# Channel mixer of a two-layer decoder on one core: order of the first half-size products' operands, of the reloads of `a`, and of the loads of the parked `x`

## The reference, cut to what matters

```python
def finish(x, m, w_o, g_post_mix, g_pre_ffn, g_post_ffn, w_gate, w_up, w_down):
    x = x + rmsnorm(m @ w_o, g_post_mix)
    h = rmsnorm(x, g_pre_ffn)
    f = (jax.nn.silu(h @ w_gate) * (h @ w_up)) @ w_down
    return x + rmsnorm(f, g_post_ffn)
```

## Time and profile before

| | |
|---|---|
| median of three executions | 3031.42 us (3029.75 to 3041.99) |
| profiled execution, its own time | 3035.28 us |
| span from first to last instruction | 3033.5 us |
| mean granted TensorE clock | 0.988 |
| TensorE (PE) busy | 2925.0 us, 96% of the span |
| VectorE (DVE) busy | 1804.6 us, 59% |
| ScalarE (ACT) busy | 1370.4 us, 45% |
| GpSimd (POOL) busy | 1169.5 us, 39% |
| half-size products, layer 0 and layer 1 | from 821 us and from 2316 us |
| down projections, layer 0 and layer 1 | from 1243 us and from 2738 us |

### The profile page before, as it was taken

The page is one execution under the profiler, slowest core; times in us unless marked ns, Lnnn a source line. Parts: engine busy times, 40 slices in busy tenths (PEclk is TensorE's granted clock), DMA queues, the critical chain, the costliest instruction groups (busy, mean ns, idle before and its releaser), DMA issues. The chain is left out here.

```text
span 3033.5 us, 53219 instructions
## 1 busy us (share of the span) xinstructions
PE 2925.0 (96%) x20726; PEld 2548.6 (84%) x20726; DVE 1804.6 (59%) x3496; ACT 1370.4 (45%) x2616; POOL 1169.5 (39%) x864
## 2 busy tenths in 40 slices
PE   8999999999899999999999999999998999998998
PEld 6777756669799999999977777665797999998997
DVE  5579675557754555444555887654678555444552
ACT  4366625564443333444333765355654333333442
POOL 3002031315465655454700201313355656654542
PEclk9999999999999999999999999999999999999999
DMA  5120325652312222676521112356512222237653
GB/s 182 40 65 29 100 100 185 232 193 60 101 57 85 85 84 73 194 215 196 150 79 46 50 34 94 142 182 232 180 60 76 77 79 82 64 115 239 186 169 103
DMA packets 391922, 357.57 MB, mean 118 GB/s; under 512 B 33281, under 2 KB 353690, under 8 KB 391674
## 3 DMA queue, kind: packets, MB, share of 16 engines
q1 hardware_dynamic: 371194, 282.86, 30.5%
q0 software_dynamic: 20480, 71.32, 6.8%
HBM read 299.66 MB, written 54.44 MB: 117 GB/s over the span
## 5 line engine op out<-in xcount | busy, mean ns | idle before, releaser
L750 PE MATMUL ps<-w_in_slots,hT 128*128 128x256 f32 (+1 forms) x2048 | 447.0, 374 | 4.9 <-PEq L214 3.2
L750 PEld LDWEIGHTS ps<-w_in_slots,hT 128*128 128x128 f32 x2048 | 373.1, 192 | 60.1 <-issue 10.2
L2901 POOL TENSOR_TENSOR t_lo<-t_raw,t_hi 128x512 fp32r<-128x512 f32 x200 | 272.6, 1365 | 259.7 <-ACT t_hi L2715 259.7
L2414 PE MATMUL ps<-a_lo,wd_hi 128*128 128x352 f32 x1056 | 348.6, 330 | 16.2 <-DVE a_lo L3057 11.7
L2414 PE MATMUL ps<-a_hi,wd_hi 128*128 128x352 f32 x1056 | 342.4, 324 | 0.0
L2414 PE MATMUL ps<-a_hi,wd_lo 128*128 128x352 f32 x1056 | 342.1, 324 | 0.0
L2929 POOL TENSOR_TENSOR wd_lo<-wd_raw,wd_hi 128x1024 fp32r<-128x1024 f32 x96 | 212.6, 2222 | 232.3 <-ACT wd_hi L2756 232.2
L3023 DVE TENSOR_TENSOR t_raw<-w_pair,w_pair 128x512 f32<-128x512 f32 x120 | 134.0, 1117 | 270.1 <-PE ps L2520 270.1
L2520 PE MATMUL ps<-s_lo,t_hi 128*128 128x264 f32 x960 | 274.9, 286 | 3.7 <-issue 3.7
L2520 PE MATMUL ps<-s_hi,t_lo 128*128 128x264 f32 x960 | 274.6, 286 | 0.0
L2520 PE MATMUL ps<-s_hi,t_hi 128*128 128x264 f32 x960 | 274.2, 286 | 0.0
(11 more groups left out here) (408 smaller groups left out, 7116.0 us busy)
## 6 DMA issues: line engine op xcount, KB each, us to landing
wd_raw<-in_w_down SPq DMA_DIRECT2D x192, 192.0 KB, 3.1
wd_raw<-in_w_down SPq DMA_DIRECT2D x96, 256.0 KB, 3.3
a_in<-apark SPq DMA_DIRECT2D x132, 176.0 KB, 3.9
w_pair<-in_w_gate SPq DMA_DIRECT2D x40, 512.0 KB, 5.1
w_pair<-in_w_up SPq DMA_DIRECT2D x40, 512.0 KB, 4.9
w_in_slots<-in_w_in SPq DMA_DIRECT2D x18, 1024.0 KB, 5.4
apark<-a SPq DMA_DIRECT2D x40, 264.0 KB, 2.1
apark<-t_up SPq DMA_DIRECT2D x40, 264.0 KB, 4.2
```

Source lines behind the costliest of these rows:

```text
L750: ins = pe.matmul(ps[:m, bank[i], 0:w], hT[:, k, cols(n)], W[:, g % 2, k, 0:w], start=(k == 0), stop=(k == KC - 1))
L2414: ins = pe.matmul(bank(b), w, x, start=first and i == 0, stop=end and i == 2)
L2901: pool.tensor_tensor(t_lo[e][:, :, :], t_raw[e][:, :, :] if len(src) > 1 else src[0], t_hi[e][:, :, :].bitcast(F32), ALU.subtract).then_in ...
```

## The change

It touches four places of `channel`. The matmuls and their order stay as they are.

1. `s5` becomes the first combination. Its sum is made by VectorE ahead of the sixth `invert` of the norm part, its rounding stands first in ScalarE's list, and its rest moves from GpSimd to VectorE. `multiply_up(2)` and `(3)` move behind the first weight sums, `multiply_up(4)` and `(5)` ahead of the rest of `s1`.
2. On ScalarE the copies of the first three products and the rounding of weight 4 move ahead of the rounding of `s7` and `s6`. On VectorE the weight sums 5, 6 and 7 are put between the last rests.
3. On SP the reloads of `a` numbers 12 to 19 move ahead of the second and third parking of the last pair and ahead of the weights of turn 1; ScalarE rounds group 0 of turn 1 after all 22 blocks of `a`.
4. The parked x comes back in 12 pieces of 128 x 2 x 352 elements, one at the end of each of the turns 3 to 6, 9 to 12 and 17 to 20, instead of three thirds in turn 2.

```diff
-    combs = {"s1": (A11, A22, ALU.add), "s5": (A11, A12, ALU.add), "s2": (A21, A22, ALU.add), "s7": (A12, A22, ALU.subtract),
+    combs = {"s5": (A11, A12, ALU.add), "s1": (A11, A22, ALU.add), "s2": (A21, A22, ALU.add), "s7": (A12, A22, ALU.subtract),
...
@@ sync
             park_pair(PAIRS - 1, 0)
+            for x in range(NX, NX + 4):
+                load_a(x)
+            park_pair(PAIRS - 1, 1)
+            for x in range(NX + 4, FC - 2):
+                load_a(x)
             sp.wait_ge(p_mm, NP - 2)
             load_down(1, 0)
-            park_pair(PAIRS - 1, 1)
-            for x in range(NX, NX + 3):
-                load_a(x)
-            load_down(1, 1)
-            load_down(1, 2)
             park_pair(PAIRS - 1, 2)
-            for x in range(NX + 3, FC - 2):
-                load_a(x)
             park_pair(PAIRS - 1, 3)
             load_a(FC - 2)
             load_a(FC - 1)
+            load_down(1, 1)
+            load_down(1, 2)
...
+            x1_at = (3, 9, 17)
...
-                if u == 2:
+                if u == x1_at[0]:
                     sp.wait_ge(p_mm, NP)
                     for n in range(3):
-                        for m in range(3):
-                            sp.wait_ge(parked[m], 32 if m == 2 else 16)
-                        sp.dma_start(third(hT, n), third(xpark, n)).then_inc(x1_in[n], 16)
+                        sp.wait_ge(parked[n], 32 if n == 2 else 16)
+                for n in range(3):
+                    if x1_at[n] <= u < x1_at[n] + 4:
+                        k = slice(2 * (u - x1_at[n]), 2 * (u - x1_at[n]) + 2)
+                        sp.dma_start(hT[:, k, of(n)], xpark[:, k, of(n)]).then_inc(x1_in[n], 16)
@@ tensor, product
-                if q == 0 and pos == 3:
-                    pe.wait_ge(s5_lo_done, 1)
-                elif q == 0 and pos >= 2:
-                    pe.wait_ge(comb_lo_done, max(1, pos - 2))
+                if q == 0 and pos >= 2:
+                    pe.wait_ge(comb_lo_done, max(2, pos - 1))
@@ scalar
+            round_comb("s5")
             silu(4)
             silu(5)
             round_comb("s1")
             for m in range(3):
                 round_weight(m)
-            round_comb("s5")
             silu(8)
             act.wait_ge(mm, 9)
             round_weight(3)
             silu(10)
-            for n in ("s2", "s7", "s6"):
+            round_comb("s2")
+            keep_product(0, 0)
+            round_weight(4)
+            keep_product(0, 1)
+            keep_product(0, 2)
+            for n in ("s7", "s6"):
                 round_comb(n)
-            for done in range(1, NP + 1):
+            for m in (5, 6):
+                round_weight(m)
+            for done in range(4, NP + 1):
...
-            round_a(0, *range(12, 15))
+            round_a(0, *range(12, FC))
             round_down(1, 0)
-            round_a(0, *range(15, FC))
@@ gpsimd
-            for m in range(3):
+            for m in range(4):
                 rest_of_weight(m)
-            pool.wait_ge(comb_hi_done, comb_nth["s5"])
-            pool.tensor_tensor(comb_lo["s5"][:, :, :], comb_raw["s5"][:, :, :], comb_hi["s5"][:, :, :].bitcast(F32), ALU.subtract).then_inc(s5_lo_done, 1)
-            rest_of_weight(3)
@@ vector
+                if th == 2:
+                    dve.wait_ge(x_add, 3 * (KC - 1))
+                    sum_comb("s5")
                 invert(2 * th + 2)
...
-            for u in range(4):
-                multiply_up(u)
+            multiply_up(0)
+            multiply_up(1)
             sum_comb("s1")
             sum_weight(0)
             sum_weight(1)
             dve.wait_ge(mm, 9)
             sum_weight(2)
-            sum_comb("s5")
-            multiply_up(4)
-            rest_of_comb("s1")
+            multiply_up(2)
+            multiply_up(3)
+            rest_of_comb("s5")
             dve.wait_ge(mm, 11)
             sum_comb("s2")
+            multiply_up(4)
             multiply_up(5)
+            rest_of_comb("s1")
             sum_comb("s7")
             sum_comb("s6")
             rest_of_comb("s2")
+            sum_weight(5)
+            rest_of_comb("s7")
+            sum_weight(6)
+            sum_weight(7)
+            rest_of_comb("s6")
```

24 lines of the change are left out of this document (10 added, 14 removed).

## The result

The changed kernel took 3007.39 us (median of four executions, 3005.28 to 3010.38) beside 3032.64 for the kernel before (four executions, 3029.75 to 3041.99): a ratio of 0.9912, 95% interval 0.9889 to 0.9936. That is 25 us or 0.9% faster, where 30.4 us were forecast. In two further groups of runs, on two chips (3 and 0), the same kernel had medians of 3005.07 and 3005.68 us (ratios 0.9900 [0.9885, 0.9916] and 0.9912 [0.9895, 0.9929]), 28.6 and 28.0 us less than the kernel before beside it. The profiled execution took 3010.38 us.

What follows compares the result with a forecast made beforehand. TensorE, busy 96% of the span, was taken to bound the kernel. Gains of 15.4 + 11.0 + 4.0 = 30.4 us, taken from the median 3031.42, gave 3001 us, range 2990 to 3014.

Steps and rivals of the forecast that it cites:

- First half-size products: Rounds 0 and 1 of these products: reordered sums and rests win 7.7 us per layer, 15.4 in both.
- The walk: New order at the half-size products stepped through with measured durations: round 1's first product ends 9.0 us earlier per layer.
- Rival A: Half-size products: VectorE's chain or the half-level clock lasts longer, 15.4 becomes 10.4, total 3006 us; chance 0.13.
- The fall: Round 0: three waits close together bring a clock fall, for which 1.3 us per layer was taken off.
- Start of the down projection: Turns 0 and 1: earlier reloads of `a` win 5.5 us per layer, 11.0 for both.
- the weights hidden, 7.9: Upper bound per layer at the down projection's start, if turn 1's first weights cause no delay: 7.9 us.
- Parked x: Down projection, turn 5: spreading the x loads removes TensorE's waits of 1.67 and 2.32 us, winning 4.0.
- rival E: Twelve pieces of x each delay a turn's weights by 2.0 us, 48 in all, total 3053 us; chance 0.03.
- Rival B: Start of the down projection gives nothing, as blocks or weights arrive late; gain 19.4, total 3012 us; chance 0.13 (with F).
- rival C: Longer VectorE chain or clock fall, and no gain at the down projection's start, together: total 3017 us; chance 0.08.
- D: More gain: round 0 without a clock fall and turn 1's weights hidden, 37 us less, total 2994; chance 0.05.

Runs made afterwards that it cites:

- u4: The changed kernel with the rest of `s5` back on GpSimd, nothing else; 3009.28 us, ratio 0.9909 to the kernel before.
- u2: The changed kernel with SP's and ScalarE's old order at the start of the down projection; 3017.77 us, ratio 0.9938 to the kernel before.
- u3: The changed kernel with the parked x loaded in three thirds in turn 2 again; 3010.86 us, ratio 0.9919 to the kernel before.
- v3: The changed kernel with the parked x in three transfers of 1408 KB, at turns 3, 9 and 17; 3013.37 us beside 3005.07 of the changed kernel.
- w4: The changed kernel with the sum of `s5` made behind the first two `multiply_up`; 3006.10 us beside 3005.68 of the changed kernel.
- v4: The changed kernel with ScalarE's three copies and weight 4's rounding behind the roundings of `s7` and `s6`; 3007.91 us beside 3005.07 of the changed kernel.
- v2: The changed kernel with turn 1's first weights loaded and rounded ahead of the reloaded blocks of `a`; 3005.10 us beside 3005.07 of the changed kernel.
- w2: A second run of the changed kernel with turn 1's first weights ahead of the reloads of `a`; 3002.91 us beside 3005.68 of the changed kernel.
- w3: The changed kernel with all twelve pieces of the parked x loaded in turn 2; 3010.37 us beside 3005.68 of the changed kernel.

## Why the prediction was right, and where it was not

**First half-size products: 15.4 forecast, 14.9 measured.** The walk held in each link that the trace shows: sum of `s5` hidden with 0.60 us to spare, three waits each 0.3 us shorter than forecast, one fall of the clock. Its two assumptions were tested apart. Rival A had the chain on VectorE longer than counted, 5 us in both layers; the waits measured say it was not, and u4 shows 2.8 us per layer for the one move. The fall was taken off at 1.3 us. The same three waits stand in 18 places (nine profiles); in 15 a fall of 3.4 us goes with them and the stretch takes 30.1 to 30.3 us, in 3 there is none (layer 0 of u2, u3 and v3) and it takes 28.7, so the fall cost 1.4. That it came in both layers of the changed kernel was likely but not certain. The walk without a fall said 9.0; 37.5 less 28.7 is 8.8. Of the 7.4 us per layer, 2.8 are the rest of `s5` (u4), 2.0 the hidden sum of `s5` (w4) and 0.7 the order of the copies with the fall it brings (v4). If these add, some 2 us are left for the moves of `multiply_up` and of the weight sums, which no run took back; the walk has them, but it is not shown.

**Start of the down projection: 11.0 forecast, 6.4 measured; this step failed.** The queues went as I had them, the wait for `wd_lo` too (2.05 for 1.9), and turn 1 started 5.4 and 5.2 us earlier for 6.0. What I left out is the clock behind that wait. I had put "turn 1 starts 6.0 us earlier" against the 31 us of the kernel before, which hold a fall of 6.8 us, and let that fall go with the waits for `a`. With the one wait of 2 us left, the clock still fell in 12 of 20 places, and in none of the four (v2, w2) where that wait was gone. That is a strong association; no run separates the wait from what came before it. Without a fall the stretch is 25.2 to 25.7 us, a gain of 5.2 to 6.0 that brackets my 5.5 and 6.0; with it the gain is 4.1 or 2.3. By the mean of the 20 places, 26.6 us, it would be about 9 us in both layers, so part of this miss is the chance of one profile. The same reasoning had been applied in round 0, where I took 1.3 us off, and was missing here. v2 shows the bound I had named, "the weights hidden, 7.9": 24.35 us, a gain of 6.9 and 6.5.

**Parked x: 4.0 forecast, 4.5 measured** by the stretch, 4.7 by w3, which puts the bytes back in one turn. Layer 1 gave more (2.6), for the same reason: in the kernel before, its wait was longer. That the pieces cost nothing in their own turns held; rival E, at 2 us for each piece, did not occur. v3 shows its mechanism with 1.4 MB in one turn beside the stores of y.

**The sum.** 30.4 forecast, 25.7 by stretches, 24.9 in the span of the profiled executions. The missing 4.7 are the second step; 0.5 too much in the first and 0.5 too little in the third cancel. Rival B (no gain there) and rival C are excluded by u2. D asked for round 0 without a fall and for hidden weights: the first occurs in 3 of 18 places, the second is v2.

## What to carry to other kernels

Price a moved wait together with the clock behind it: a new wait of 2 us on the engine that bounds the kernel came here with 1.4 to 3.2 us more in 12 of 20 places (against the 25.4 that the others take on average) and with nothing in 8, so compare stretches between marks before medians. When two engines take turns on operands, give the work to the one that holds them for the shorter time, and fill its idle time ahead of a dependency with sums that are needed later. A transfer for which nobody waits is priced by what is queued behind it: spread it in pieces over stretches that have slack, above all away from those in which results are stored.

## What the runs showed that I had not expected

The same 2.05 to 2.07 us wait at the same matmul came with a fall to 1.2 GHz in 12 of 20 places and with none in 8, and the time of the kernel with that wait removed is not clearly shorter: the granted clock of its executions is 0.990 to 0.993, that of the changed kernel 0.991 to 0.995. What decides whether a fall comes stays open.

A transfer of 1408 KB took 11.1 us to land beside weights and stores, where the 345 GB/s of the earlier trace rows give 4.1 to 4.2, and one of 352 KB 4.9 at the same place, where they give 1.0. The estimate from a mean rate was short by more than half. The DMA engines moved 3.93 MB in those 16 us (v3, 2912 to 2928), 2.5 MB of it other data, so the transfer shared them; how much of the 11.1 us that explains no run shows.
